# Two weight units at a time behind a norm, three slots of weights and three pairs of banks

## The reference, cut to what matters

```python
def rms_norm(x, gain):
    x32 = x.astype(jnp.float32)
    y = x32 * lax.rsqrt(jnp.mean(x32 * x32, axis=-1, keepdims=True) + RMS_EPS) * gain.astype(jnp.float32)
    return y.astype(x.dtype)

def swiglu(h, w_gate, w_up, w_down):
    return (jax.nn.silu(h @ w_gate) * (h @ w_up)) @ w_down

# first block, for l in 0, 1 (D_FF = 4096)
    h = rmsnorm(x, norm1_g[l])
    u = h @ w_in[l]                      # 1032 + 1536 + 1024 columns
    mix = concat(mlstm_mixer(u), diff_attention(u), hgrn2_mixer(u))
    x = x + mix @ w_out[l]
    x = x + square(relu(rmsnorm(x, norm2_g[l]) @ w_up[l])) @ w_down[l]

# second block, for layer in 0, 1 (inner width 2816)
    f = swiglu(rms_norm(h, g[0]), ...);  h = h + 0.5 * rms_norm(f, g[1])
    hm = rms_norm(h, g[2])
    mix = pool_mixer(hm, ...) if layer == 0 else dilated_mixer(hm, ..., k_sh, v_sh, ...)
    h = h + rms_norm(mix, g[3])
    f = swiglu(rms_norm(h, g[4]), ...);  h = h + 0.5 * rms_norm(f, g[5])
    if layer == 0:
        k_sh, v_sh = shared_kv(h, ...)   # both from rms_norm(h, kv_gain)
```

## Time and profile before

| | |
|---|---|
| median of 3 runs | 3775.18 us (3771.95 to 3777.56) |
| the profiled execution | 3776.8 us |
| its span | 3775.5 us |
| PE busy | 3446.4 us, 91% of the span |
| DVE, ACT, POOL busy | 1345.3, 1133.3, 1221.2 us |
| POOL's weight subtraction L413 | 288 times, 4198 ns in the mean |
| mean granted clock of TensorE | 0.937 of full speed |

### The profile page before, as it was taken

One profiled execution on the slowest core, in us unless ns is written; L12 is line 12 of the kernel. 1 busy time (PEld: TensorE's weight loads), 2 busy tenths in 40 slices (PEclk: granted clock), 3 DMA queues, 4 the chain that ended last, 5 costly groups with the idle time before them and its releaser, 6 DMA issues.

```text
span 3775.5 us, 37038 instructions
## 1 busy us (share of the span) xinstructions
PE 3446.4 (91%) x15554; PEld 2738.6 (73%) x15554; DVE 1345.3 (36%) x2176; ACT 1133.3 (30%) x1553; POOL 1221.2 (32%) x300
## 2 busy tenths in 40 slices
PE   7887799998977999999998789998999988769999
PEld 5654588886744688888886678886888866647887
DVE  4436541324256431222125542124221254573122
ACT  2234332322234332332223232223222233422222
POOL 4210044443300243444442334433444431014442
PEclk9987799999978899999999899999999989779999
DMA  3210033232200133333332223333433332013332
GB/s 120 61 52 1 12 101 99 91 101 67 69 28 1 56 90 100 96 94 92 99 90 80 81 73 92 98 92 111 132 95 96 87 105 84 1 39 89 101 96 72
DMA packets 462182, 296.75 MB, mean 79 GB/s; under 512 B 14330, under 2 KB 454192, under 8 KB 462016
## 3 DMA queue, kind: packets, MB, share of 16 engines
q1 hardware_dynamic: 453664, 277.09, 25.2%
q10 hardware_dynamic: 8352, 17.30, 1.3%
HBM read 285.97 MB, written 8.39 MB: 78 GB/s over the span
## 4 chain that ended last, share of the span: by engine, by line
PE 82%; DVE 13%; ACT 3%; issue 1%; POOL 0%; SPq 0%; DMA 0%; ACTq 0%; DVEq 0%
PE bank L473 24%; PE bank L474 24%; PE bank L475 24%; PE bank L313 9%; DVE x L778 1%; DVE ta L776 1%; DVE ta L539 1%; DVE ta L1160 1%; DVE xl L801 1%; POOL wlo L413 0%; DVE qkv L1942 0%; DVE u L1456 0%; DVE ta L1939 0%; DVE scr L1697 0%; DVE sqacc L795 0%
## 5 line engine op out<-in xcount | busy, mean ns | idle before, releaser
L413 POOL TENSOR_TENSOR wlo<-raw,whi 128x2048 fp32r<-128x2048 f32 (+3 forms) x288 | 1208.8, 4198 | 2519.6 <-ACT whi L406 2519.6
L473 PE MATMUL bank<-xh,whi 128*128 128x512 f32 x2432 | 972.8, 400 | 68.5 <-DVE xl L801 37.6
L474 PE MATMUL bank<-xl,whi 128*128 128x512 f32 x2432 | 958.9, 394 | 0.0
L475 PE MATMUL bank<-xh,wlo 128*128 128x512 f32 x2432 | 958.3, 394 | 0.0
L406 ACT ACTIVATE whi<-raw 128x2048 fp32r<-128x2048 f32 (+3 forms) x288 | 503.4, 1748 | 685.0 <-PE bank L475 650.1
L473 PEld LDWEIGHTS bank<-xh,whi 128*128 128x128 f32 x2432 | 464.6, 191 | 184.9 <-POOL wlo L413 33.2
L475 PEld LDWEIGHTS bank<-xh,wlo 128*128 128x128 f32 x2432 | 463.8, 191 | 99.1
L474 PEld LDWEIGHTS bank<-xl,whi 128*128 128x128 f32 x2432 | 465.1, 191 | 93.3
L473 PE MATMUL bank<-ah,whi 128*128 128x512 f32 x1216 | 473.0, 389 | 0.0
L474 PE MATMUL bank<-al,whi 128*128 128x512 f32 x1216 | 473.0, 389 | 0.0
L475 PE MATMUL bank<-ah,wlo 128*128 128x512 f32 x1216 | 473.0, 389 | 0.0
(11 more groups left out here) (339 smaller groups left out, 3043.6 us busy)
## 6 DMA issues: line engine op xcount, KB each, us to landing
raw<-in_ffn_w_gate SPq DMA_DIRECT2D x88, 512.0 KB, 4.0
raw<-in_ffn_w_up SPq DMA_DIRECT2D x88, 512.0 KB, 5.3
raw<-in_w_up SPq DMA_DIRECT2D x64, 512.0 KB, 4.8
raw<-in_w_down SPq DMA_DIRECT2D x64, 512.0 KB, 4.8
raw<-in_w_in SPq DMA_DIRECT2D x56, 512.0 KB, 4.8
raw<-in_ffn_w_down SPq DMA_DIRECT2D x64, 384.0 KB, 4.0
raw<-in_ffn_w_down SPq DMA_DIRECT2D x64, 320.0 KB, 3.5
raw<-in_w_out SPq DMA_DIRECT2D x16, 512.0 KB, 4.1
```

Source lines behind the costliest of these rows:

```text
L413: g.e.tensor_tensor(self.wlo[slot][:, 0:n], self.raw[slot][:, 0:n], self.whi[slot][:, 0:n].bitcast(F32), ALU.subtract).then_inc(self.lo_ma ...
L473: pe.e.matmul(bank, hi[:, at:at + P], xh, start=k == ks[0], stop=False)
L474: pe.e.matmul(bank, hi[:, at:at + P], xl, start=False, stop=False)
L475: last = pe.e.matmul(bank, lo[:, at:at + P], xh, start=False, stop=k == ks[-1])
```

## The change

Four things are changed.

First, the first two units of each of the ten normed phases are multiplied together: for each K tile PE does both output tiles of unit 0 and both of unit 1, 96 matmuls in all, into four banks. The sum of squares follows after both, and the spread after the fourth chunk of the third unit (for `q` at once).

Second, `whi` has three slots, and `raw` and `wlo` share three more: GpSimd writes the rest in place over the loaded weights. A slot is loaded when the unit three before has been multiplied. `act_hi` and `pool_lo` run two units ahead. In the dense phases PSUM is used in three pairs of banks (0 to 5); in the phases named in `NARROW` in two.

Third, the factors of every norm are spread from the columns, as the post norms did it; the four multiplications by the identity are gone.

Fourth, for the third unit of the five phases behind a post norm, GpSimd subtracts in two halves and only after DVE has finished that norm's squares. Of the gates' weights only the eight used columns per K tile are rounded and subtracted.

```diff
+NARROW = ("gates", "in_ah", "out", "q", "o")
+def first_banks():
+    at, before, last, base = [], [], {}, 4
+    for u, ph in enumerate(UNITS):
+        narrow = ph.name.rstrip("01") in NARROW
+        base = (base + 2) % (4 if narrow else 6)
+        at.append(base)
+        before.append(last.get(base))
+        last[base] = u
+    return at, before
+FIRST_BANK, BANKS_BEFORE = first_banks()
+def in_halves(u):
+    return u < len(UNITS) and UNITS[u].name in ("pool_in", "gateupb0", "k", "q", "gateupd0") and u == UNITS[u].first + 2
+def steps_of(ph, j):
+    if ph.norm and j < 2:
+        return 0 if j else 2 * ph.nk * ph.tiles
+    return ph.nk * ph.tiles if ph.tiles else 1
...
-        self.raw = [at(f"raw{s}", [P, SLOT], F32, offset=RING_AT + s * SLOT * 4) for s in range(2)]
-        self.whi = [at(f"whi{s}", [P, SLOT], F32R, offset=RING_AT + (2 + s) * SLOT * 4) for s in range(2)]
-        self.wlo = [at(f"wlo{s}", [P, SLOT], F32R, offset=RING_AT + (4 + s) * SLOT * 4) for s in range(2)]
+        self.raw = [at(f"raw{s}", [P, SLOT], F32, offset=RING_AT + s * SLOT * 4) for s in range(3)]
+        self.wlo = [at(f"wlo{s}", [P, SLOT], F32R, offset=RING_AT + s * SLOT * 4) for s in range(3)]
+        self.whi = [at(f"whi{s}", [P, SLOT], F32R, offset=RING_AT + (3 + s) * SLOT * 4) for s in range(3)]
...
-        if u >= 2:
-            sp.wait_ge(self.lo_made, self.lo_made[u - 2])
+        if u >= 3:
+            sp.wait_ge(self.tile_done, self.tile_done[u - 3])
...
     def act_hi(self, u):
+        if u >= 3:
+            a.wait_ge(self.tile_done, self.tile_done[u - 3])
         a.wait_ge(self.raw_landed[slot], self.raw_landed[slot][u])
-        if u >= 2:
-            a.wait_ge(self.tile_done, self.tile_done[u - 2])
...
     def pool_lo(self, u):
         g.wait_ge(self.hi_made, self.hi_made[u])
+        if in_halves(u):
+            g.wait_ge(self.part_v, self.part_v["squares of", ph.name])
+            for t in range(2):
+                raw_t, hi_t, lo_t = [w.rearrange("p (k s n) -> p k s n", s=2, n=P)[:, :, t, :] for w in (raw, hi, lo)]
+                g.e.tensor_tensor(lo_t, raw_t, hi_t.bitcast(F32), ALU.subtract).then_inc(self.lo_made.tick(u, t), 1)
...
+    def pe_two_units(self, ph, ks):
+        for j in range(2):
+            self.pe_unit_ready(ph.first + j)
+        for k in ks:
+            self.pe_operand(ph.name, 0, k)
+            xh, xl = self.operand(ph.name, 0, k)
+            for j in range(2):
+                u, hi, lo = ph.first + j, self.whi[(ph.first + j) % 3], self.wlo[(ph.first + j) % 3]
+                for t in range(2):
+                    at, bank = (2 * k + t) * P, self.bank[FIRST_BANK[u] + t][:]
+                    pe.e.matmul(bank, hi[:, at:at + P], xh, start=k == ks[0], stop=False)
+                    pe.e.matmul(bank, hi[:, at:at + P], xl, start=False, stop=False)
+                    last = pe.e.matmul(bank, lo[:, at:at + P], xh, start=False, stop=k == ks[-1])
...
     def pe_spread(self):
-        pe.wait_ge(self.norm_v, self.norm_v["diagonal", n])
+        pe.wait_ge(self.norm_v, self.norm_v["factors", n])
         for b in range(NB):
-            last = self.mm(spread[:, b * P:b * P + P], self.ones[:], self.ta[0][:, b * P:b * P + P], b == 0, b == NB - 1)
+            last = self.mm(spread[:, b * P:b * P + P], self.tiny[:, 8 + b:9 + b].to_broadcast([P, P]), self.c(C_IDENT), b == 0, b == NB - 1)
...
     def dve_norm(self):
-        v.e.reciprocal(t[:, 8:12], t[:, 4:8]).then_inc(self.norm_v.tick(), 1)
-        for b in range(NB):
-            last = v.e.tensor_scalar(self.ta[0][:, b * P:b * P + P], self.c(C_IDENT), t[:, 8 + b:9 + b], None, ALU.mult)
+        self.dve_factors()
         v.e.tensor_copy(self.rs[:], self.bank[7][:]).then_inc(self.norm_v.tick("rs", n), 1)
...
     def act_dense(self, name):
-            self.act_hi(u + 1)
-            for _ in range(ph.nk * ph.tiles if ph.tiles else 1):
-                yield
+            steps = steps_of(ph, j)
+            late = ph.evac.startswith("f") and ph.evac.endswith("last") and j == ph.count - 1
+            ahead = [] if late or in_halves(u + 2) else [u + 2]
+            for n in range(steps):
+                if n == steps // 2 and ahead:
+                    self.act_hi(ahead.pop())
+                yield
+            if ahead:
+                self.act_hi(ahead.pop())
             if j == 0 and ph.norm:
                 self.act_norm()
-                self.act_hi(u + 2)
             for t in range(ph.tiles):
                 self.act_tile(ph, j, t)
+            if late:
+                self.act_hi(u + 2)
...
     def act_post_norm(self, gain, next_gain):
         for j in range(KC):
+            if j == 4:
+                self.act_hi(next_unit + 2)
```

96 lines of the change are left out of this document (54 added, 42 removed).

## The result

The changed kernel takes 3807.1 us (median of 4 runs, 3806.5 to 3807.6) against 3776.1 for the kernel before on the same chips: ratio 1.0081, 95% interval 1.0069 to 1.0093. It is 31 us slower where I had forecast 12.8 faster, and outside my range. The profiled execution has a span of 3806.3 us against 3775.5, with a granted TensorE clock of 0.929 against 0.937 in the mean.

The account below looks back on a forecast made before the run. PE, busy in 91% of the span, was taken as the bound, with gains only at entrances, `pool_group`, start and mixers. Won 35.3 less lost 22.5 gave net 12.8 us: 3776.8 to 3764.0 (3762 on the median's scale), range 3750 to 3774.

Parts of the forecast that it names:

- part 2: Rounding moved into post norms: entrances 1.7 to 2.6 us later; last step, `q`: PE sets the pace, 11 us won.
- the attention's chain binds: Rival in `q`: the attention's chain is the limit, so the 10.9 us stay; 3773 us, chance 0.12.
- part 4: The rest: start 1 us lost, small waits 3 us won, mixers 0 with bounds 8 either side for both layers.
- one place of the post norm: DVE's L778, held by GpSimd's subtraction in the post norm, waits 0.8 us.
- My slower rival: Mixers: ACT held waiting for loads, 1.3 us at each of 20 `in_ah` units, 26 us; 3788 us, chance 0.13.
- the two units at the entrances: Behind post norms: pairing ends PE's waits for `xl` between K tiles; `gateupb0` near 138 us, `k` near 69.
- the later entrances: Behind post norms: starts later by 2.6 (`pool_in`), 1.7 (`gateupb0`), 1.9 (`k`), 2.1 us (`q`).
- the late fourth unit with its clock: At `up00`: PE waits 4.3 us for the fourth unit's weights, lower clock costs 2.4; phase about 97 us.
- the start: Kernel start: ACT waits for the second load and GpSimd's subtraction falls on DVE's first `xl`; 1 us lost.
- `gateupd0`'s entrance: Start of `gateupd0` behind its post norm: 2.3 us later, an estimate.
- `pool_in` with what follows: `pool_in` and `pool_group`: factors 2.2 us later, shorter GpSimd wait at the last units; 1 us won, bounds 8 won, 4 lost.
- the excess: Time of phases behind post norms above PE's own pace: 15.2 us at `gateupb0`, 14.8 at `k` and `gateupd0`, mostly removed by pairing.

Follow-up runs that it names:

- the pairing-undone kernel: Changed kernel with the first two units of `q` one after the other again, sum and spread behind the first: 3792.8 us, ratio 1.0052 to the kernel before.
- the early tables: Changed kernel, `q` still paired, with its positions fetched as the preceding post norm ends and its sine tables made ahead of the factors: 3791.1 us, ratio 1.0043.
- the columns alone: Kernel before with only the factors spread from the column of reciprocals, DVE's four identity products gone: 3768.0 us, ratio 0.9984.
- the last kernel: Changed kernel with pairs only at `in_m0`, `gateupb0`, `k`, `gateupd0`, roundings of `in_ah` and `q` in their old place, some others moved: 3733.7 us, ratio 0.9891.
- the short subtraction: Changed kernel with GpSimd subtracting only 128 columns in `in_ah` and `q`'s fourth and fifth units, leaving out part of the computation: 3786.9 us, ratio 1.0026.
- the old place: Changed kernel with ACT's mixer roundings back where the kernel before had them (unit u+1 at the start of unit u): 3798.5 us, ratio 1.0060.

## Why the prediction was wrong

**The step that failed** is the last of part 2: "PE sets the pace, and 10.9 us go; 11 won", with bounds "nothing ... and 12". I took the busy share of PE in a window (85.2 of 92.9 us) for the limit. The pace is that of the attention's chain; the pairing-undone kernel is back at 266.7 us from `q` to `o`, 17 us less, although it weaves 48 matmuls more, and the early tables get as much back with the pair. The rival "the attention's chain binds" named the mechanism and priced it at 0 instead of a loss, since I did not ask when its first instruction could run. It costs 4.3 us by positions that are fetched in a burst, and 8.5 by holds. The remaining 4 us of the 17.3, after the rotations, I can't assign. The attention alone alternates at 9 and 14 us from step to step in the paired kernels and goes at 10 in the others, but that isn't the reason: the early tables show the same alternation and take 223.1 us from the rotations to `o`, as the unpaired kernel does. And measured from the columns alone (260.7) the loss is larger than from the kernel before: about 6 us more belong to the moved roundings of `q`, which the last kernel gets back by their old place.

**The second** is part 4: "The mixers keep their instructions ... I take 0". In part 2 I had the very row, L636 with 4.57 us, and applied it to one place of the post norm. The twenty roundings that moved in `in_ah` are twenty subtractions of 4.5 us that moved, and some of them fell on the chain of the gates, for which PE waits (L1218 in both layers, L1622 in layer 0): 11.5 us lost, beyond my 8. With the short subtraction 14.0 us come back in the two layers, with the old place 10.6; the first is more than was lost, since it also shortens a hold that the kernel before had in each layer. My slower rival put the loss here, but by ACT waiting for loads; it was the hold, at a few places and not at each unit.

**Right, with its size:** the two units at the entrances (`gateupb0` 139.2 for 138, `k` 70.0 for 69, no wait between K tiles), the later entrances (2.7, 1.5, 2.0, 2.2 us for 2.6, 1.7, 1.9, 2.1), the late fourth unit with its clock (`up00` 94.9 for 97, as less stands inside it and more ahead of it: 7.2 for 7.8 together), the start. **Off in size:** `gateupd0`'s entrance 4.0 us later for 2.3. `pool_in` with what follows 4.2 won for 1, inside my bounds, but not for my reasons: I gave it no late fourth unit, and there PE waits 7.12 us; the pair costs 4.0 us and the rest of the change wins more than that. And the gain of a pair itself is 4.5 us, not the 10 that the excess suggested: the other 6.1 us of `gateupb0` come without a pair, most likely by the second unit's weights, whose wait of 3.2 us and its lower clock go. The sum hid this, since both were in the change.

**The held instruction.** The timeline shows L1218 held for 4.24 us and the kernel with the short subtraction shows the hold shrink with GpSimd's time. The Trainium skill (SBUF — State Buffer, section on the two separate sides) says that whoever starts first has the pair for the whole instruction and that a DVE operation with two SBUF inputs is concerned; the traces agree. So the rule was known to me, and the fault was to apply it to the places I looked at and not to all that the change moves.
